# Two buffer pairs for the turned inner activations of an expert, and the last chunk's turn one unit earlier

## What is computed

```python
def swiglu(h, w_in, w_out):
    g, u = jnp.split(jnp.einsum('bld,df->blf', h, w_in), 2, axis=-1)
    return jnp.einsum('blf,fd->bld', jax.nn.silu(g) * u, w_out)

def moe_swiglu(h, w_router, w_exp_in, w_exp_out):
    logits = jnp.einsum('bld,de->ble', h, w_router).astype(jnp.float32)
    top_v, top_i = lax.top_k(logits, TOP_K)
    gates = jax.nn.softmax(top_v, axis=-1)
    dense_gate = jnp.sum(jax.nn.one_hot(top_i, N_EXPERTS, dtype=jnp.float32) * gates[..., None], axis=-2)
    y = jnp.zeros_like(h)
    for e in range(N_EXPERTS):
        y = y + dense_gate[..., e:e + 1] * swiglu(h, w_exp_in[e], w_exp_out[e])
    return y
```

## Time and profile before

| | us |
|---|---|
| runs | 1982.80, 1991.99, 1983.13 |
| median | 1983.13 |
| the profiled execution | 1999.38 |
| its span | 1997.6 |
| TensorE busy (share of the span) | 1858.6 (93%) |
| VectorE busy | 1346.4 (67%) |
| ScalarE busy | 1046.4 (52%) |
| mean granted clock of TensorE | 0.943 |

### The profile page before, as it was taken

How to read it: one execution, slowest core, us unless ns; L and a number is a source line. 1 busy time by engine, 2 the same in 40 slices (tenths; PEclk the granted TensorE clock), 3 DMA queues, 4 the chain that set the end, 5 groups by cost and what they waited for, 6 DMA issues and landing times.

```text
span 1997.6 us, 25921 instructions
## 1 busy us (share of the span) xinstructions
PE 1858.6 (93%) x9997; PEld 1610.9 (81%) x9997; DVE 1346.4 (67%) x1177; ACT 1046.4 (52%) x913; POOL 76.6 (4%) x85
## 2 busy tenths in 40 slices
PE   5999988998989989887999999999999999999995
PEld 4988877998979978676887878878788788787884
DVE  3636544444346355546987879888888898887986
ACT  3443223333234433124676766767677667676674
POOL 2002120000000021200000000000000000000000
PEclk8997879999989979697999999999999999999997
DMA  7432143443443421243998999999999999899992
GB/s 235 147 109 53 38 115 109 153 150 102 134 153 123 131 51 37 53 148 123 339 361 301 357 327 341 363 315 351 339 327 360 320 348 362 313 345 334 343 361 83
DMA packets 267757, 452.11 MB, mean 226 GB/s; under 512 B 41242, under 2 KB 102930, under 8 KB 267688
## 3 DMA queue, kind: packets, MB, share of 16 engines
q1 hardware_dynamic: 265824, 447.51, 65.3%
q0 software_dynamic: 1600, 3.46, 0.8%
q10 hardware_dynamic: 264, 0.17, 0.0%
HBM read 440.14 MB, written 10.97 MB: 226 GB/s over the span
## 4 chain that ended last, share of the span: by engine, by line
PE 87%; DVE 8%; ACT 3%; issue 1%; DMA 1%; DVEq 0%; POOL 0%; SPq 0%; ACTq 0%
PE ps L1472 15%; PE ps L1473 15%; PE ps L1998 10%; PE ps L1467 7%; PE ps L1468 7%; PE ps L2012 5%; PE ps L1546 3%; PE ps L1912 3%; PE ps L1653 3%; PE ps L1638 2%; DVE cvt L1017 1%; PE ps L1927 1%; PE ps L1808 1%; DVE spL L915 1%; PE ps L2040 1%
## 5 line engine op out<-in xcount | busy, mean ns | idle before, releaser
L1363 DVE TENSOR_TENSOR spL<-ring,spH 128x2048 fp32r<-128x2048 f32 x339 | 771.9, 2292 | 154.1 <-ACT spH L846 154.0
L846 ACT ACTIVATE spH<-ring 128x2048 fp32r<-128x2048 f32 x339 | 648.3, 1915 | 164.4 <-PE ps L2012 102.5
L1472 PE MATMUL ps<-spH,XH 128*128 128x512 f32 x896 | 357.8, 399 | 1.5 <-DVE XL L1375 1.5
L1473 PE MATMUL ps<-spH,XL 128*128 128x512 f32 x896 | 352.5, 393 | 0.0
L915 DVE TENSOR_TENSOR spL<-ring,spH 128x2048 fp32r<-128x2048 f32 (+1 forms) x74 | 158.4, 2147 | 238.2 <-ACT spH L571 238.2
L1467 PE MATMUL ps<-hnH,spH 128*128 128x320 f32 x928 | 275.7, 312 | 13.7 <-DVE hnL L933 7.1
L1468 PE MATMUL ps<-hnL,spH 128*128 128x320 f32 x928 | 274.1, 310 | 0.0
L571 ACT ACTIVATE spH<-ring 128x2048 fp32r<-128x2048 f32 (+1 forms) x74 | 132.7, 1798 | 247.6 <-PE ps L1546 108.6
L1998 PE MATMUL ps<-spL,XH 128*128 128x512 f32 x896 | 242.4, 392 | 0.0
L1472 PEld LDWEIGHTS ps<-spH,XH 128*128 128x128 f32 x896 | 168.9, 189 | 38.6 <-issue 1.7
L1998 PEld LDWEIGHTS ps<-spL,XH 128*128 128x128 f32 x896 | 168.8, 188 | 37.7
(11 more groups left out here) (321 smaller groups left out, 2120.4 us busy)
## 6 DMA issues: line engine op xcount, KB each, us to landing
ring<-in_w_exp_in_dram SPq DMA_DIRECT2D x227, 1024.0 KB, 7.3
ring<-in_w_exp_out_dram SPq DMA_DIRECT2D x112, 1024.0 KB, 7.3
ring<-in_w_in_dram SPq DMA_DIRECT2D x28, 1024.0 KB, 5.9
ring<-in_w_ffn_in_dram SPq DMA_DIRECT2D x22, 1024.0 KB, 5.1
ring<-in_w_ffn_out_dram SPq DMA_DIRECT2D x16, 704.0 KB, 4.6
ring<-in_w_out_dram SPq DMA_DIRECT2D x8, 1024.0 KB, 5.1
out_dram<-ring SPq DMA_DIRECT2D x32, 256.0 KB, 2.6
ring<-in_state_hgrn_dram SPq DMA_DIRECT2D x16, 256.0 KB, 3.9
```

The costliest lines, as they stand in the source:

```text
L846: A(esplit(j)[0], src, ACT.Copy).then_inc(S("hi_done"), 1)
L1363: V.tensor_tensor(lo, eslot(j)[0], hi.bitcast(F32), ALU.subtract).then_inc(S("split_done"), 1)
L1472: mm(out, x[0], w, start=start, stop=False)
L1473: return mm(out, x[1], w, start=False, stop=False)
```

## The change

There are two pairs of `hTH` and `hTL`. Even chunks use the old pair and odd chunks a new one, which lies over `xT`, at the start of the kernel's buffers. The turn of chunk 6 moves from behind unit 39 to behind unit 38, between the two down units of chunk 5. Nothing else moves; no instruction is added or taken away.

```diff
-TURN_AT = [EXPERT_UNITS.index(("up", c + 1, 1)) for c in range(EC - 1)] + [EXPERT_UNITS.index(("down", EC - 2, 1))]
+TURN_AT = [EXPERT_UNITS.index(("up", c + 1, 1)) for c in range(EC - 1)] + [EXPERT_UNITS.index(("down", EC - 2, 0))]
...
         hTH = put("hTH", [P, 4, P], F32R)
         hTL = put("hTL", [P, 4, P], F32R)
+        hT2 = [(hTH, hTL), (put("hTH1", [P, 4, P], F32R, offset=base), put("hTL1", [P, 4, P], F32R, offset=base + 2048))]
...
                         act.wait_ge(S("eh_tr"), it * EC + (c + 1))
-                        A(hTH[:], ps[:, 4, :].rearrange("p (k n) -> p k n", k=4), ACT.Copy
+                        A(hT2[c % 2][0][:], ps[:, 4, :].rearrange("p (k n) -> p k n", k=4), ACT.Copy
                           ).then_inc(S("hTH_done"), 1)
...
                         dve.wait_ge(S("hTH_done"), it * EC + (c + 1))
-                        V.tensor_tensor(hTL[:], ps[:, 4, :].rearrange("p (k n) -> p k n", k=4), hTH[:].bitcast(F32),
-                                        ALU.subtract).then_inc(S("hTL_done"), 1)
+                        V.tensor_tensor(hT2[c % 2][1][:], ps[:, 4, :].rearrange("p (k n) -> p k n", k=4),
+                                        hT2[c % 2][0][:].bitcast(F32), ALU.subtract).then_inc(S("hTL_done"), 1)
...
                         if i == 0:
                             pe.wait_ge(S("hTL_done"), it * EC + (c + 1))
+                        tH, tL = hT2[c % 2]
                         for k in range(2):
                             f = 2 * i + k
                             for q in range(2):
-                                highx(ps[:, 6 + q, :], (hTH[:, f], hTL[:, f]), wH[:, k, 512 * q:512 * q + 512],
+                                highx(ps[:, 6 + q, :], (tH[:, f], tL[:, f]), wH[:, k, 512 * q:512 * q + 512],
                                       start=c == 0 and f == 0)
                         pe.wait_ge(S("split_done"), it * EU + (U0 + j + 1))
                         for k in range(2):
                             f = 2 * i + k
                             for q in range(2):
-                                m = mm(ps[:, 6 + q, :], hTH[:, f], wL[:, k, 512 * q:512 * q + 512],
+                                m = mm(ps[:, 6 + q, :], tH[:, f], wL[:, k, 512 * q:512 * q + 512],
                                        start=False, stop=c == EC - 1 and f == 3)
```

## The result

The changed kernel takes 1976.6 us, the median of 16 runs (1965.59 to 1983.84). The kernel before takes 1995.63 us, the median of 16 runs (1982.80 to 2001.59), among them the three known when the forecast was made, whose median was 1983.13. The ratio is 0.9909, with a 95% interval of 0.9893 to 0.9926: faster by 0.7 to 1.1%, or 15 to 21 us. The forecast was 1965.4 us with a range up to 1973.5, so the time lies outside the range, while the saving of the forecast, 17.7 of 1983.13 us, is a ratio of 0.9911.

A forecast was written before the change was run, and what follows sets the result against it. TensorE was taken to bound the kernel, stalling once per expert for hTL. Stall 16.2 us plus clock 1.5 us gave 17.7 us, off the median 1983.13: 1965.4 us, range 1961.5 to 1973.5.

The forecast's parts named there:

- The start of the sum: Whole kernel: the saving of 17.7 us taken off the median of the runs, 1983.13 us, giving 1965.4 us.
- some scatter: Upper end of the range, 1973.5 us: allowance because one of three runs lay 9 us over the others.
- The stall: TensorE before unit 40 waits for hTL once per expert: 2.02 us, eight times, 16.2 us saved; lower bound 14.4.
- The measure from start to start: At unit 40, product starts with and without the stall are compared: 2.02 us each, against 1.79 in the wait view.
- the view of waits: Profile view of TensorE's waits for hTL in the loop: 8 times, 14.4 us, taken as the stall's lower bound.
- The clock: Half-clock drop behind the first expert's stall goes with the hole: 1.5 us saved, bounded by 0 and 12 us.
- The chain's margin: Moved turn of chunk 6: unit 40 may begin from 1184.12 and comes at 1184.89, leaving 0.77 us.
- The rival of a part-time stall: Moved chain before unit 40 takes about 0.5 us more than its cover; 4 us remain, 1969.5 us; chance 0.09.
- The split of unit 41: ScalarE and VectorE split unit 41 later, behind the moved turn; margins 2.9 us (high half), 2.5 us (low).
- The second pair at cost 0: Chunks 1, 3 and 5 write another address, over xT: cost 0, bounded by 0.1 us in a covered product or copy.
- The loads: Expert loads in the loop meet 345 GB/s without binding; rival that they bind: 1980 us, chance 0.06.
- one by one: Expert loads: the skill's 341 GB/s for 1 MB read as single transfers; by that rule time stays at 1983.

The follow-up runs named there:

- the changed kernel with four copies: Changed kernel plus four ScalarE copies into unread buffers ahead of chunk 6's copy to hTH: 1982.78 us, ratio 0.9944 to the kernel before.
- The longer stall: Kernel before plus four ScalarE copies into unread buffers ahead of chunk 6's copy to hTH: 2018.33 us, ratio 1.0124 to the kernel before.
- the pairs alone: Two buffer pairs, with chunk 6's turn left behind unit 39, against the kernel before: 1997.95 us, ratio 1.0017.

## Why the prediction was right and where it went wrong

**The start of the sum failed.** The step was: "The median of the runs, 1983.13, is 16.2 us below that execution, which I can't place; the stalls have fixed length, so I take the saving off whole". The saving was right within what the runs can tell, the number it was taken from wasn't the kernel's time. Three runs had given 1982.80, 1991.99 and 1983.13. With 16 the median is 1995.63, and 1995.63 - 17.7 = 1977.9 lies 1.3 us from the measured 1976.6. That the ratios agree to 0.0002 is luck in part, since the interval of the measured one spans 6.6 us and the saving in the loop's trace was 19.1, not 17.7. The other number at hand, the profiled execution less the saving, was 1981.7, and its counterpart measured 1978.76. The range took in "some scatter" at its upper end, but 1999.38 beside a median of 1983 was a sign that the scatter was of the size of the effect.

**Where the scatter lies.** In the traces it is ahead of the loop. The loop of one kernel repeats within 0.1 us (1039.9 and 1040.0 before, 1020.8 to 1020.9 after; 0.2 with both pairs over xT), while its start ranges from 920.7 to 929.7 us over the 13 traces of the two kernels and their variants, whose work up to there is the same. The clock goes with it: over the 16 runs of the changed kernel the shortest span, 1963.8 us, has a mean granted clock of 0.953, the longest, 1982.1, one of 0.944; of the 23 runs of the kernel before in the first series the one at 1982.96 us has 0.954, the highest of all, where the median run has 0.948. Two traces show it for the first 900 us, the first of a loop that starts at 929.7 (the kernel before), the second at 920.7 (the changed kernel with four copies):

```profile
0.00:900.00 900.00, 811.24 (x5204) 754.20 (x5204) 423.68 (x534) 304.35 (x401) 74.39 (x81) 0.90 0.37 113
0.00:900.00 900.00, 808.38 (x5231) 751.28 (x5231) 429.32 (x554) 309.13 (x409) 74.33 (x81) 0.92 0.38 113
```

This is a connection, not an experiment on it; why an execution gets less of the full clock there stays open, and no trace of a run near 1983 of the kernel before was taken.

**The stall.** Right in place, kind and size. The starts in the trace gave 2.02 us each, 16.2 in all; the waits are gone and an expert takes 127.33 us instead of 129.55, so 2.22 less, of which the move has 2.07 and the second pair 0.15. The measure from start to start is borne out: with the 14.4 us of the view of waits, 1.8 us more of the 19.1 would be without a name.

**The clock.** 1.5 us for the one drop behind the first stall was right for the profiled execution, and the second trace of the kernel before has the same drop. The longer stall shows that such holes bring drops; how many there are in the runs of which no trace was kept isn't known.

**The chain's margin.** Called 0.77 us, measured 1.09. The step took 0.33 us between the copy's end and the subtraction as the engine's own delay. It was VectorE still at the split of unit 41; without that in the way the gap is 0.03 us (1177.18 against 1177.15). The rival of a part-time stall had its place on this margin and needed 0.3 us more than it was given.

**The split of unit 41.** Right: its high half starts at 1177.04, 1.13 us behind the transposes, as worked out (0.63 + 0.50), and nobody waits.

**The second pair at cost 0.** Off by a small gain: 1.1 us of loop by the trace of the pairs alone. With it the terms come to 16.2 + 1.5 + 1.1 = 18.8 of the 19.1 us measured in the loop; with 16.5 for the move, as measured against the two pairs alone, they come to 19.1.

**The loads.** They don't bind. The rates of the two stretches above are 343 and 347 GB/s, where 345 were asked for, with landings of 7.2 us at the median and 11.6 at most, and no wait for one. The Trainium skill ("DMA: Bandwidth & Descriptors", section Measured) lists 341 GB/s for a DMA of 1 MB issued from GpSimd. The row gives one size of transfer, and the prediction's "one by one" is a reading of it; as a limit on these loads, issued from SyncE with several in flight, it doesn't hold in the trace, by the 343 and 347 above and the 353 and 355 of the earlier trace rows.

## What to carry over

Where the bounding engine is busy but for one hole per pass, move the producer's step ahead by one unit of other work: that is worth the whole hole, and the chain from producer to reader, taken from start to start, says how much cover it needs. Here that was 2.07 us per expert, and a margin of 1.09 us was left. A gap between two steps of a chain can be another job of the engine, so read its other work beside it before pricing the chain. A trace forecasts the difference well, but the absolute time only as well as its start is known: where the profiled execution and the median of a few runs stand apart by as much as the effect, the range has to reach from the one to the other.

## What the runs showed of the hardware

- Holes of 2.07 to 2.10 us in TensorE's work brought the granted clock down to half (2.4 to 1.2 GHz) behind 3 of 24, holes of 3.73 us behind 7 of 8, at 1.5 us each; holes of 1.11 us behind none of 8. So a hole of these lengths can cost more than its length.
- The place of a 4 KB pair of buffers moved the spacing of the 512-column products that read it by 1.3 ns (233.5 to 232.2) and that of the up products, which don't, by 0.4 ns on average, 2.5 to 2.7 us over the loop.
- Copies of 128 x 512 on ScalarE take 0.60 us each, but the next work of the engine begins 0.50 us behind the start of one: four of them delayed the next by 1.93 us.
